# First attention layer: the first transposes of blocks 6 and 7 placed inside the next turn's gate piece and token tile

## The chip, the cores and the metric

The kernel runs on one core of a Trainium2 chip. The metric is the device time of one execution in microseconds (us), taken as the median of several runs. Engines are named as in the profile: PE (matrix multiply), PEld (its weight loads), DVE (vector), ACT (scalar), POOL (GpSimd) and SP (the queue that issues the DMAs).

## The reference

Two groups of rows, a prompt of 1024 positions and a sample of 32 with 512 cached positions, go through two layers that share the weights. The change lies in the first layer's mixer, a differential attention. Cut to what matters here (8 heads of 2 x 64, `h` the normalised input):

```python
q, k, v, g = jnp.split(h @ w_in, 4, axis=-1)
q = _rope(q.reshape(b, t, A_HEADS, 2, A_DH), pos)
k = _rope(k.reshape(b, t, A_HEADS, 2, A_DH), pos)
...
s = jnp.einsum('bqhcd,bkhcd->bhcqk', qb, kf) * (A_DH ** -0.5)
mask = k_chunk[None, :] <= (qpb // CHUNK)[:, None]
pr = jax.nn.softmax(jnp.where(mask, s, NEG_INF), axis=-1)
w = pr[:, :, 0] - lam * pr[:, :, 1]
o = jnp.einsum('bhqk,bkhe->bqhe', w, vf)
...
o = _rmsnorm(o, sub_g) * (1.0 - lam_init)
o = o.reshape(b, t, A_WIDTH) * jax.nn.silu(g)
```

The output projection, a gated addition of a second input, a second layer of another kind of attention with the same additions, and a final normalisation follow. The change touches none of these.

## The kernel before

`diff_layer` runs eight head groups one after another (`groups`, `body(r, more)`, where `more` is false in the last). Each engine has its own program, and the engines meet at semaphores alone. Within a group every program walks through the same turns, `for j in range(2, LAST + 1)` with `LAST = 13`. A turn carries pieces of different stages of the pipeline, written out by hand in a fixed order per engine.

There are nine units u: eight blocks of 128 query rows (0 to 7; block u sees (u + 1) x 128 keys) and the sample (8). For each unit the work passes through these steps:

- `scores(u)` on PE, in turn u + 2;
- `maxima(u)` on DVE and `probs(u, c)` on ACT (exponentials of the two softmaxes), in turn u + 3;
- `combine(u)` on DVE (L655): it scales the second softmax (L663) and adds the first to it (L665, SCALAR_TENSOR_TENSOR), which is the tile `la_p`. The semaphore `weights` tells that it is done;
- `turn_weights(u, g)` on PE (L855, instruction line L868): it transposes `la_p` in sets of up to four 128 x 128 pieces into one PSUM bank, `la_third`. Set g = 0 stood at the end of turn u + 4, set g = 1 (blocks 4 to 7 alone have one) in the middle of turn u + 5;
- `move(u, g)` on ACT (L459, line L473): it copies the bank to `la_wt`. The next set waits for that (`moved`), since there is only one bank;
- `values(c)` on PE (L871, line L892): weights times values, for blocks 0 to 3 in turn 8, for blocks 4 to 7 at the end of turn 12, and for the sample in turn 13.

To give PE work between these steps, turns 9 to 11 also carry the gate's projection (`gate_project(c, ks)`, L905: three column pieces of 352, each with eight steps `ks` of three matmuls at L107 on `la_wg_high` and `la_wg_low`), and turns 12 and 13 carry the next group's first two token tiles (`project(ahead, t, ks)`, L794: eight steps of three matmuls at L107 on `area`). Both are cut into `EARLY` (steps 0 to 4) and `LATE` (steps 5 to 7), and other work stands between the two. In the last group there is no next tile.

The next tile's weights come into `area` in two parts while the group runs: ACT rounds a slice (L427), then POOL forms the rest (`split_w`, L773). Steps 0 to 2 are split in turn 9, 3 to 5 in turn 10, 6 and 7 in turn 11. `project(ahead, 0, ...)` waits before each of its steps k for POOL's split of that step. POOL also multiplies the gate (`gate_product(c)`, L769), in turns 10 to 12 and ahead of that turn's splits; it waits for ACT's last gate step (`gate_sigmoid`, L492), which waits for DVE's `gate_soft(c)` (L689), which stands behind `combine` in DVE's program. ACT's order in turn 11 is: the sample's exponentials, `move(6, 1)`, `gate_log(1)`, `gate_raw(2)`, `gate_sigmoid(1)`, `move(7, 0)`, the rounding of slices 6 and 7. In turn 12: `move(7, 1)`, `gate_log(2)`, `gate_sigmoid(2)`, `move(8, 0)`. DVE's in turn 12: the clamp of gate piece 2, `combine(8)`, `gate_soft(2)`, `finish(0)` (L677).

In the last group ACT and DVE split the first two blocks of the output weights in place of the next tile's slices (`OUT_AT`, turns 9 and 10; ACT L562, DVE L713), on ACT directly behind that turn's `move(j - 4, 0)`.

Of the kernel before, what the change touches and what calls it, by code (L numbers as in the profile page):

```python
# [32 lines left out]
NT = SEQ // P  # L33
# [69 lines left out]
def three(pe, out, a, b, start, stop, **kw):  # L103

    pairs = [(a[0], b[0]), (a[1], b[0]), (a[0], b[1])]
    for n, (x, y) in enumerate(pairs):
        last = pe.matmul(out, x, y, start=start and n == 0, stop=stop and n == 2, **kw)  # L107
    return last
# [153 lines left out]
def diff_layer(nc, top, name, h, w_in, k_past, v_past, k_out, v_out, o_dram, w_out, ident, neg_lam, gain, cos, sin, stage, area, pj):  # L262
# [7 lines left out]
    GATE_AT = {9: 0, 10: 1, 11: 2}  # L270
# [7 lines left out]
    def groups_of(u):  # L278

        if u == NT:  # L280
            return [(0, PB + 1)]
        return [(k, min(4, u + 1 - k)) for k in range(0, u + 1, 4)]
# [4 lines left out]
    with ExitStack() as ctx:  # L287
# [503 lines left out]
        def _(pe):  # L791
            start_credits(pe, {x: s for x, s in S.items() if x != "w_low"}, 4, 5)

            def project(at, t, ks):  # L794
                n = TILES[t][1]
                rows = slice(t * P, t * P + n)
                for k in ks:
                    if t == 0:
                        pe.wait_ge(S["w_low"], at.nth("w_low", k + 1))
                    last = three(pe, pj[0:n, t % 2, 0:NQ], [x[:, k, rows] for x in h], [x[:, k, :] for x in w],  # L800
                                 k == 0, k == KT - 1, skip_group_check=True)
                if ks[-1] == KT - 1:
                    last.then_inc(S["pj_tok"], 1)

            def turn(at, t):
                pe.wait_ge(S["rope"], at.nth("rope", t + 1))
                n = TILES[t][1]
                if n < P:
                    pe.sem_inc(S["pe_tick"], 1)
                for x in range(2):  # L810
                    last = pe.transpose(pj[:, t % 2, x * P:x * P + n], tok[0:n, t, x * P:(x + 1) * P], ident[0:n, 0:n])
                last.then_inc(S["turned"], 1)

            EARLY, LATE = range(0, 5), range(5, KT)
# [9 lines left out]
            def body(r, more):  # L824
                at, ahead = Count(table, r), Count(table, r + 1)
# [29 lines left out]
                def turn_weights(u, g):  # L855
                    q0, n, nk = UNITS[u]
                    pe.wait_ge(S["weights"], at.nth("weights", u + 1))
                    pe.wait_ge(S["moved"], at.nth("moved", moves_before(u) + g))
                    if u == 0:
                        pe.wait_ge(S["log"], at.before("log"))  # L860
                    if n < P:
                        pe.sem_inc(S["pe_tick"], 1)
                    k0, nb = groups_of(u)[g]
                    bank = third[:, 0:nb * n].rearrange("p (b n) -> p b n", n=n)
                    for b in range(nb):
                        k = (k0 + b) * P
                        rows = min(P, nk - k)
                        last = pe.transpose(bank[0:rows, b, :], p[0][u % 3][0:n, k:k + rows], ident[0:n, 0:n])  # L868
                    last.then_inc(S["w_turned"], 1)

                def values(c):  # L871
                    c0, cn = CHUNKS[c]

                    if c == 0:
                        pe.wait_ge(S["normed"], at.before("normed"))
                    elif c == 1:
                        pe.wait_ge(S["normed"], at.nth("normed", 1))
                    else:
                        pe.wait_ge(S["probs"], at.all("probs"))

                    pe.wait_ge(S["moved"], at.nth("moved", moves_before((4, 8, 9)[c])))
                    out = sums_bank(c)
                    if c == 2:
                        for b in range(PB):
                            pe.matmul(out[:, 0:cn], vp[:, b, :], wt_sample[:, b, :], start=b == 0, stop=False)
                        last = pe.matmul(out[:, 0:cn], tok[0:DEC, NT, 2 * P:], wt_sample[0:DEC, PB, :],
                                         start=False, stop=True)
                    else:
                        blocks = 4 * (c + 1)
                        for b in range(blocks):  # L890
                            q = max(0, b * P - c0)
                            last = pe.matmul(out[:, q:], tok[:, b, 2 * P:], wt[:, b, q:],  # L892
                                             start=b == 0, stop=b == blocks - 1)
                    last.then_inc(S["pv"], 1)

                def variance(c):
                    cn = CHUNKS[c][1]
                    pe.wait_ge(S["squared"], at.nth("squared", c + 1))
                    if c == 0:
                        pe.wait_ge(S["turned_low"], at.all("turned_low"))  # L900
                    elif c == 1:
                        pe.wait_ge(S["moved"], at.all("moved"))
                    pe.matmul(var_bank(c)[:, 0:cn], mean[:, :], squares(c), start=True, stop=True).then_inc(S["var"], 1)

                def gate_project(c, ks):  # L905
                    if ks[0] == 0:
                        if c == 0:
                            pe.wait_ge(S["gw_low"], at.all("gw_low"))
                            pe.wait_ge(S["turned_low"], at.nth("turned_low", NT))
                        elif c == 1:  # L910
                            pe.wait_ge(S["log"], at.nth("log", 1))
                        else:
                            pe.wait_ge(S["g_raw"], at.nth("g_raw", 1))
                    for k in ks:
                        last = three(pe, gate_bank(c), [x[:, k, :] for x in wg],
                                     [x[:, k, gate_cols(c)] for x in h], k == 0, k == KT - 1, skip_group_check=True)
                    if ks[-1] == KT - 1:
                        last.then_inc(S["g_ready"], 1)

                def free_bank(t):  # L920

                    if t < 2:
                        pe.wait_ge(S["g_raw"], at.nth("g_raw", t + 2))
                    else:
                        pe.wait_ge(S["turned_low"], at.nth("turned_low", t - 1))
                    if t == PAST_AT + 1:
                        pe.wait_ge(S["past_low"], at.all("past_low"))

                for j in range(2, LAST + 1):
                    if j <= 8:  # L930
                        free_bank(j)
                        project(at, j, EARLY)
                    if j in GATE_AT:
                        gate_project(GATE_AT[j], EARLY)
                    if more and j >= 12:
                        free_bank(j - 12)
                        project(ahead, j - 12, EARLY)
                    if j <= 9:
                        turn(at, j - 1)
                    if more and j == 13:  # L940
                        turn(ahead, 0)
                    if 0 <= j - 5 <= NT and len(groups_of(j - 5)) > 1:
                        turn_weights(j - 5, 1)
                    if j == 13:
                        values(2)
                    if j <= 8:
                        project(at, j, LATE)
                    if j in GATE_AT:
                        gate_project(GATE_AT[j], LATE)
                    if more and j >= 12:  # L950
                        project(ahead, j - 12, LATE)
                    if j == PAST_AT:
                        pe.wait_ge(S["past"], at.nth("past", 32))
                        pe.wait_ge(S["turned_low"], at.nth("turned_low", PAST_AT))
                        for b in range(PB):
                            last = pe.transpose(past_bank[:, b * P:(b + 1) * P], kp[:, b, :], ident[:, :])
                        last.then_inc(S["past_turned"], 1)
                    if j == 9:
                        variance(0)
                    if 0 <= j - 2 <= NT:  # L960
                        scores(j - 2)
                    if 0 <= j - 4 <= NT:
                        turn_weights(j - 4, 0)
                    if j == 8:
                        values(0)
                    if j == 12:
                        values(1)
# [1389 lines left out]
```

## Time and profile before

| | |
|---|---|
| median of 3 runs | 2026.64 us |
| lowest and highest | 2021.52 and 2026.65 us |
| the profiled execution, whole time | 2027.47 us |
| its span | 2025.6 us (1.87 us of its time lie around it) |
| PE busy, share of the span | 1897.3 us, 94% |
| DVE, ACT, POOL busy | 1122.7, 1069.4, 387.3 us |
| mean granted TensorE clock | 0.975 of full speed |

The eight groups of the first attention lie at about 60 to 710 us of the span, and follow each other every 81.2 us. In the windows of 80 us between 80 and 640 us, PE is busy for 77.4 of 80 us and the granted clock is 1.00.

In the rows, times are us from the span's start; a timeline row gives start, duration, engine, line, operation, output <- inputs, shapes and count, and in brackets the engine's idle time just before and what ended it. Matmuls overlap, so the distance from one start to the next tells their price. A matmul's modelled end and POOL's spans are rough.

### The profile page before, as it was taken

How to read it: one execution, taken by the hardware profiler on the slowest of the kernel's cores; microseconds unless marked ns; L12 is line 12 of the kernel's file. 1: busy time of each engine (PE TensorE's matmuls, PEld its weight loads, DVE VectorE, ACT ScalarE, POOL GpSimd, SP SyncE). 2: the span in 40 equal slices, each digit the busy share in tenths (PEclk: the TensorE clock that was granted, in tenths of full speed). 3: DMA queues.
4: the chain of work that ended last, by engine and by line, in shares of the span. 5: the costliest groups of instructions: out<-in, count | busy, mean ns of one | idle time of the engine just before them, and what ended most of it. 6: DMA issues, size and time to landing. Idle time of an engine off the chain costs nothing. (4 is left out here: it accounts for less than half of the span.)

```text
span 2025.6 us, 31736 instructions
## 1 busy us (share of the span) xinstructions
PE 1897.3 (94%) x11429; PEld 1623.9 (80%) x11429; DVE 1122.7 (55%) x2269; ACT 1069.4 (53%) x2556; POOL 387.3 (19%) x597
## 2 busy tenths in 40 slices
PE   4999999999999899997799999999999999889996
PEld 4887878878878699986678787878787778689995
DVE  5556455565564532455165657575657575753555
ACT  5456455454554522454266667566657575732335
POOL 0132222321322000265001111110111011100341
PEclk7999999999999899998899999999999999999999
DMA  4121112111211242211111111111101111243113
GB/s 153 55 66 38 48 51 61 59 49 51 72 38 48 97 122 81 68 63 49 52 48 37 49 38 48 38 48 38 56 30 59 31 55 45 80 125 95 53 52 125
DMA packets 161803, 125.07 MB, mean 62 GB/s; under 512 B 10992, under 2 KB 152624, under 8 KB 161648
## 3 DMA queue, kind: packets, MB, share of 16 engines
q1 hardware_dynamic: 160784, 122.85, 19.8%
q8 instruction: 92, 1.51, 0.3%
q14 instruction: 63, 0.52, 0.1%
q10 hardware_dynamic: 864, 0.20, 0.0%
HBM read 89.49 MB, written 33.52 MB: 61 GB/s over the span
## 5 line engine op out<-in xcount | busy, mean ns | idle before, releaser
L107 PE MATMUL pj<-area,h_high 128*128 128x384 f32 (+1 forms) x2304 | 660.9, 349 | 25.8 <-issue 11.3
L107 PEld LDWEIGHTS pj<-area,h_high 128*128 128x128 f32 (+1 forms) x2304 | 408.2, 181 | 49.2 <-issue 11.4
L107 PE MATMUL pj<-area,h_low 128*128 128x384 f32 (+1 forms) x1152 | 390.8, 339 | 0.0
L107 PEld LDWEIGHTS pj<-area,h_low 128*128 128x128 f32 (+1 forms) x1152 | 210.3, 183 | 8.5
L1530 POOL TENSOR_TENSOR lb_o<-lb_o,lb_keep 128x512 f32<-128x512 f32 (+3 forms) x80 | 77.2, 965 | 603.0 <-ACT lb_keep L1230 596.4
L1375 DVE SCALAR_TENSOR_TENSOR lb_s<-lb_sc,lb_m 128x512 f32<-128x512 f32 (+4 forms) x200 | 109.9, 550 | 73.9 <-ACT lb_m L1211 73.9
L1201 ACT ACTIVATE lb_m<-lb_sc 128x512 f32<-128x512 f32 (+4 forms) x200 | 87.7, 486 | 81.0 <-PE lb_sc L1612 41.0
L455 ACT ACTIVATE la_p<-la_sc,la_nm 128x128 f32<-128x128 f32 (+5 forms) x144 | 105.8, 737 | 33.8 <-DVE la_nm L652 32.9
L1406 DVE CAST lb_s_high<-lb_s 128x512 fp32r<-128x512 f32 (+1 forms) x192 | 105.5, 549 | 25.7 <-DVE lb_s L1375 0.5
L1408 DVE TENSOR_TENSOR lb_s_low<-lb_s,lb_s_high 128x512 fp32r<-128x512 f32 (+1 forms) x192 | 115.5, 601 | 6.6
L650 DVE TENSOR_REDUCE la_mx<-la_sc 128x1 f32<-128x128 f32 (+5 forms) x144 | 107.6, 747 | 2.2
L1425 DVE TENSOR_TENSOR lb_o<-lb_acc,lb_o 128x512 f32<-128x512 f32 (+3 forms) x80 | 42.3, 529 | 112.8 <-PE lb_acc L1670 112.1
L107 PE MATMUL pj<-h_high,area 128*128 128x384 f32 (+1 forms) x384 | 94.4, 331 | 6.0 <-PEq L93 4.7
L1186 ACT ACTIVATE lb_tok<-pj,norm_token 128x128 f32<-128x128 f32 (+1 forms) x72 | 26.4, 367 | 133.2 <-PE pj L107 133.2
L1634 PEld LDWEIGHTS lb_sc<-lb_s_high,lb_tri 128*128 128x128 f32 x192 | 36.4, 189 | 73.6 <-issue 70.1
L1206 ACT ACTIVATE lb_m<-lb_m 128x512 f32<-128x512 f32 (+4 forms) x200 | 93.8, 522 | 0.3
L1211 ACT ACTIVATE lb_m<-lb_m 128x512 f32<-128x512 f32 (+4 forms) x200 | 93.6, 520 | 0.3
L1221 ACT ACTIVATE lb_a<-lb_sc 128x512 f32<-128x512 f32 (+4 forms) x200 | 87.8, 489 | 7.8 <-PE lb_sc L1634 5.9
L107 PE MATMUL mix_b_g<-mix_b_x_high,area 128*128 128x384 f32 (+1 forms) x384 | 91.7, 324 | 0.0
L107 PE MATMUL mix_a_g<-mix_a_x_high,area 128*128 128x384 f32 (+1 forms) x384 | 91.3, 323 | 0.0
L1634 PE MATMUL lb_sc<-lb_s_high,lb_tri 128*128 128x512 f32 (+1 forms) x192 | 76.6, 407 | 13.6 <-DVE lb_s_low L1408 13.5
L757 POOL TENSOR_TENSOR la_ra<-la_tok,cos 128x64 f32<-128x64 f32 (+1 forms) x72 | 23.1, 321 | 335.6 <-ACT la_tok L438 335.6
(307 smaller groups left out, 4491.7 us busy)
## 6 DMA issues: line engine op xcount, KB each, us to landing
stage<-in_a_w_in SPq DMA_DIRECT2D x60, 192.0 KB, 3.5
stage<-in_b_w_in SPq DMA_DIRECT2D x60, 192.0 KB, 3.0
stage<-in_ple_w_gate SPq DMA_DIRECT2D x22, 512.0 KB, 3.8
h_low<-o_t SPq DMA_DIRECT2D x14, 528.0 KB, 6.2
mix_b_xs<-x_mid SPq DMA_DIRECT2D x8, 528.0 KB
lift_xt<-in_x SPq DMA_DIRECT2D x8, 512.0 KB, 4.4
stage<-in_a_w_in SPq DMA_DIRECT2D x16, 256.0 KB, 5.1
out_ak<-la_tok SPq DMA_DIRECT2D x8, 512.0 KB, 3.3
```

What stands on the lines that cost most here:

```text
L107: last = pe.matmul(out, x, y, start=start and n == 0, stop=stop and n == 2, **kw)
L455: act.activation(p[c][u % (3 - c)][0:n, 0:nk], scores_of(u)[:, c, :], ACT.Exp, bias=nm[0:n, u % 2, c:c + 1], accum_out=sums[0:n, u % 2, c: ...
L650: dve.reduce_max(mx[0:n, u % 2, c:c + 1], x[:, c, :], AX.X).then_inc(S["dve_link"], 1)
L1201: act.activation(x, slot, ACT.Abs).then_inc(S["size"], 1)
L1206: act.activation(x, x, ACT.Exp, scale=-1.0).then_inc(S["exp"], 1)
L1211: act.activation(x, x, ACT.Ln, bias=1.0).then_inc(S["log"], 1)
L1221: act.activation(a, slot, ACT.Exp).then_inc(S["a"], 1)
L1375: ins = dve.scalar_tensor_tensor(out=sp, in0=slot, scalar=0.0, in1=x, op0=ALU.max, op1=ALU.add)
L1406: dve.tensor_copy(high, sp).then_inc(S["high"], 1)
L1408: dve.tensor_tensor(low, sp, high.bitcast(F32), ALU.subtract).then_inc(S["low"], 1)
L1530: pool.tensor_tensor(out, out, kept[n % 2][:, q:], ALU.mult).then_inc(S["scaled"], 1)
L1634: last = pe.matmul(slot, tri[:, :], part, **add)
```

## The change

The set g = 0 of block 6 moves from the end of turn 10 to turn 11, behind the first two steps of gate piece 2; that of block 7 moves from the end of turn 11 to turn 12, behind the first three steps of the next group's tile 0 (in the last group to the start of turn 12, with nothing ahead of it). Only PE's program differs; the other engines' programs, all waits and all buffers are as they were.

```diff
-                    if j in GATE_AT:
+                    if j in GATE_AT and j != 11:
                         gate_project(GATE_AT[j], EARLY)
-                    if more and j >= 12:
-                        free_bank(j - 12)
-                        project(ahead, j - 12, EARLY)
+                    if j == 11:
+                        gate_project(GATE_AT[j], EARLY[0:2])
+                        turn_weights(6, 0)
+                        gate_project(GATE_AT[j], EARLY[2:])
+                    if j == 12:
+                        if more:
+                            free_bank(0)
+                            project(ahead, 0, EARLY[0:3])
+                        turn_weights(7, 0)
+                        if more:
+                            project(ahead, 0, EARLY[3:])
+                    if more and j == 13:
+                        free_bank(1)
+                        project(ahead, 1, EARLY)
...
-                    if 0 <= j - 4 <= NT:
+                    if 0 <= j - 4 <= NT and j - 4 not in (6, 7):
                         turn_weights(j - 4, 0)
```

On PE, at the border of turns 10 and 11 of the first group, where `la_sc` is the sample's scores, `la_p00` the weights of block 6 and `la_wg` the gate's weights:

```order
 L851 MATMUL la_sc<-la_qk_low,la_qk_high 32x32 x2
+L107 MATMUL pj<-h_high,la_wg_high 128x352
+L107 MATMUL pj<-h_high,la_wg_low 128x352
+L107 MATMUL pj<-h_low,la_wg_high 128x352
+L107 MATMUL pj<-h_high,la_wg_high 128x352
+L107 MATMUL pj<-h_high,la_wg_low 128x352
+L107 MATMUL pj<-h_low,la_wg_high 128x352
 L868 MATMUL la_third<-ident,la_p00 128x128 x4
```

Six matmuls of the gate now stand ahead of block 6's four transposes instead of behind them; this is so in all eight groups.

On PE, at the border of turns 11 and 12 of the first group, where `la_p10` is the weights of block 7 and `area` the next group's projection weights:

```order
 L107 MATMUL pj<-h_low,la_wg_high 128x352
+L107 MATMUL pj<-area,h_high 128x384
+L107 MATMUL pj<-area,h_low 128x384
+L107 MATMUL pj<-area,h_high 128x384 x2
+L107 MATMUL pj<-area,h_low 128x384
+L107 MATMUL pj<-area,h_high 128x384 x2
+L107 MATMUL pj<-area,h_low 128x384
+L107 MATMUL pj<-area,h_high 128x384
 L868 MATMUL la_third<-ident,la_p10 128x128 x4
 L107 MATMUL pj<-area,h_high 128x384
```

Nine matmuls of the next tile now stand ahead of block 7's first four transposes, in seven groups. Steps 3 to 7 of that tile, block 7's second set and the sample's set follow in the order they had.

On PE of the changed kernel, at the border of turns 11 and 12 of the last group, where `la_p20` is the sample's weights:

```order
L107 MATMUL pj<-h_low,la_wg_high 128x352
L868 MATMUL la_third<-ident,la_p10 128x128 x8
L868 MATMUL la_third<-ident,la_p20 128x32 x4
L868 MATMUL la_third<-ident,la_p20 32x32
L892 MATMUL la_acc<-la_wt,la_tok 128x512 x5
```

Here block 7's two sets stand behind the gate's last matmul with nothing between or ahead of them, as they did before.

## Rows read from the trace of the kernel before

**Rows 1.** The page, busy time, share and instructions of each engine
```profile
PE 1897.3 (94%) x11429; PEld 1623.9 (80%) x11429; DVE 1122.7 (55%) x2269; ACT 1069.4 (53%) x2556; POOL 387.3 (19%) x597
```

**Rows 2.** PE's waits, 60 to 710 us: total, times, longest
```profile
PE la_third L868 <- DVE la_p L665: 19.6, 16, 1.7
```

**Rows 3.** Timeline of PE, second group, turns 10 to 12
```profile
193.75 0.66 PE L868 MATMUL la_third<-ident,la_p 128*128 128x128 f32 x4 [0.74 <-DVE la_p L665]
...
200.28 0.66 PE L868 MATMUL la_third<-ident,la_p 128*128 128x128 f32 x4 [1.70 <-DVE la_p L665]
200.69 0.42 PE L107 MATMUL pj<-area,h_high 128*128 128x384 f32 x1
...
202.53 0.34 PE L107 MATMUL pj<-area,h_low 128*128 128x384 f32 x1
...
204.72 0.64 PE L107 MATMUL pj<-area,h_high 128*128 128x384 f32 x2
...
205.64 0.46 PE L868 MATMUL la_third<-ident,la_p 32*128 32x32 f32 x5
```

**Rows 4.** Timeline of PEld, second group, tile 0's last step
```profile
204.92 0.19 PEld L107 LDWEIGHTS pj<-area,h_high 128*128 128x128 f32 x1 [0.18 <-POOL area L773]
```

**Rows 5.** Tile `area`, PEld, 60 to 700 us: idle until, total, times
```profile
  POOL area L773: 1.1, 7
```

**Rows 6.** Timeline of POOL, second group, turns 10 to 12
```profile
195.65 3.50 POOL L773 TENSOR_TENSOR area<-stage,area 128x384 fp32r<-128x384 f32 x3
...
201.27 0.95 POOL L769 TENSOR_TENSOR la_gate<-la_gate,la_gtmp 128x352 f32<-128x352 f32 x1 [2.12 <-ACT la_gtmp L492]
202.18 1.22 POOL L773 TENSOR_TENSOR area<-stage,area 128x384 fp32r<-128x384 f32 x1
...
203.36 1.50 POOL L773 TENSOR_TENSOR area<-stage,area 128x384 fp32r<-128x384 f32 x1
```

**Rows 7.** Timeline of DVE, second group, turns 11 and 12
```profile
198.32 1.91 DVE L665 SCALAR_TENSOR_TENSOR la_p<-la_p,la_sums 128x1024 f32<-128x1024 f32 x1
200.15 0.51 DVE L689 SCALAR_TENSOR_TENSOR la_gtmp<-la_gate,la_gtmp 128x352 f32<-128x352 f32 x1
...
202.55 1.43 DVE L665 SCALAR_TENSOR_TENSOR la_p<-la_p,la_sums 32x544 f32<-32x544 f32 x1
205.59 0.53 DVE L689 SCALAR_TENSOR_TENSOR la_gtmp<-la_gate,la_gtmp 128x352 f32<-128x352 f32 x1 [1.61 <-ACT la_gtmp L487]
```

**Rows 8.** Timeline of ACT, second group, turns 10 to 12
```profile
194.57 0.58 ACT L473 ACTIVATE la_wt<-la_third 128x512 f32<-128x512 f32 x1
...
200.70 0.50 ACT L492 ACTIVATE la_gtmp<-la_gtmp 128x352 f32<-128x352 f32 x1 [1.29 <-DVE la_gtmp L689]
...
201.58 0.93 ACT L427 ACTIVATE area<-stage 128x384 fp32r<-128x384 f32 x2
204.04 0.60 ACT L473 ACTIVATE la_wt<-la_third 128x512 f32<-128x512 f32 x1 [1.53 <-PE la_third L868]
```

**Rows 9.** Timelines of PE, ACT and DVE, last group, turns 10 to 12
```profile
684.80 0.64 PE L107 MATMUL pj<-h_high,la_wg_high 128*128 128x352 f32 x1
...
686.71 0.49 PE L107 MATMUL pj<-h_high,la_wg_high 128*128 128x352 f32 x1
...
692.36 0.66 PE L868 MATMUL la_third<-ident,la_p 128*128 128x128 f32 x4 [1.44 <-DVE la_p L665]
...
696.11 8.85 PE L892 MATMUL la_acc<-la_wt,la_tok 128*128 128x512 f32 x16
...
685.18 0.60 ACT L473 ACTIVATE la_wt<-la_third 128x512 f32<-128x512 f32 x1 [0.57 <-PE la_third L868]
...
686.76 1.23 DVE L713 TENSOR_TENSOR area<-stage,area 128x1024 fp32r<-128x1024 f32 x1 [2.08 <-ACT area L562]
...
691.02 1.28 DVE L665 SCALAR_TENSOR_TENSOR la_p<-la_p,la_sums 128x1024 f32<-128x1024 f32 x1
```

**Rows 10.** Stretch of the last group: length; busy PE, PEld, DVE, ACT, POOL; clock; DMA
```profile
695.35:702.18 6.83, 6.66 (x12) 3.05 (x13) 3.65 (x5) 3.37 (x7) 0.93 (x1) 0.50 0.95 387
```

## The prediction

> **What bounds the kernel now.** I read the page's busy times first: PE is at work for 94% of the span [rows 1], so little can be won by moving PE's own work, and the question is what PE waits for. The waits of PE over the first attention answer it: it stands still in front of the transposes L868 until DVE's L665 has finished a block's weights, 16 times, 19.6 us in all [rows 2]. The timeline of PE shows which: in each of the eight groups block 6's first set waits about 0.74 us and block 7's about 1.70 us [rows 3]; eight times 2.44 is the 19.5 us. So the edit aims at the right place, and its ceiling is 19.6 us, 1.0% of the time.
>
> Next I ask what else ends late just behind that place. The weight loads of PE show a short wait there, 0.18 us for POOL's split L773, in front of the last step (k = 7) of the next group's tile 0 [rows 4]. Summed over the layer it is only 1.1 us, but there are seven of them, one for every group that has a next tile [rows 5]. POOL's last split ends at 203.36 + 1.50 = 204.86 and the load starts at 204.92 [rows 4, 6]. PE reaches its step 7 just as POOL releases it. This small row decides the case: whatever PE gains ahead of step 7 is given back in front of it, unless POOL's split comes earlier as well.
>
> Does it? The chain behind it can be followed through three engines. DVE ends block 7's L665 at 198.32 + 1.91 = 200.23 and then runs the gate's L689 until 200.66 [rows 7]; ACT's L492 starts at 200.70 [rows 8]; POOL's product L769 at 201.27, and its two splits at 202.18 and 203.36 [rows 6]. The transposes that PE waits for hang on the same 200.23 (they start at 200.28). So PE's stall and POOL's split have one origin, DVE's chain, which starts from scores that PE computes well ahead of the moved pieces. Nothing in the change makes this chain start earlier.
>
> **The change part by part, groups with a next tile (seven).** *Block 6's set.* PE is done with the sample's scores at 193.75 - 0.74 = 193.01 and now does six gate matmuls first. The same six take 1.91 us in the last group, where the clock is half [rows 9], so about 0.96 here, and the set starts at about 194.0, with its input ready: the wait of 0.74 is gone. *Block 7's set.* All PE work up to it is 0.74 earlier, so PE would stand at 200.28 - 1.70 - 0.74 = 197.84 where it stood at 198.58. Nine matmuls of tile 0 come next. From 200.69 to 202.53 there are ten distances of 0.184 us [rows 3], so nine cost 1.66, and the set is reached at 199.50. Its input is there at 200.28 as before, so 0.78 us of wait remain. PE is then 1.66 us ahead: the ceiling for these groups is 7 x 1.66 = 11.6 us, not 17.
>
> *Behind it.* Steps 3 and 4, block 7's second set and step 5 follow at once. Step 6 needs the first of POOL's last two splits (ends about 203.4), step 7 the second (204.86). Tile 0's last first matmul came at about 204.90 before [rows 3, 4] and comes at 204.92 now: the 1.66 us are spent there, in two waits of PE for POOL. From the sample's set at 205.64 on [rows 3] all is as it was, and the period of 81.2 us stays. Value taken: 0, with the bounds 0 (POOL holds exactly) and -1.66 (POOL does not hold).
>
> *A price on the way.* Block 6's first set ends at about 194.0 + 0.66 = 194.7, and ACT's copy of it, which started at 194.57 [rows 8], starts 0.1 us later. Behind the copy ACT rounds slices 3 to 5, and POOL's three splits at 195.65 [rows 6] follow it. They run beside block 7's `combine`, and its L665 takes 1.91 us here [rows 7] against 1.28 in the last group, where POOL splits nothing [rows 9]. So a shift of POOL can become a shift of DVE's chain, and that sets step 7. Bounds 0 and 0.3 us (the whole shift of the transposes); I take 0.1, since ACT was busy until 194.57 anyway: 7 x 0.1 = 0.7 us.
>
> **The last group.** There is no next tile, so block 7's set gets nothing in front of it and its wait for DVE stays. But block 6's set is moved behind six matmuls at half clock, 686.71 - 684.80 = 1.91 us [rows 9]. ACT's copy waits for PE there (0.57 us, at 685.18); behind it ACT rounds the output weights, and DVE waits 2.08 us for that at 686.76, ahead of block 7's `combine` at 691.02 [rows 9]. None of these has slack, so block 7's set moves from 692.36 to 694.3 and the values from 696.11 to 698.0. The values run at half clock until 702.18 [rows 10]; starting 1.9 later, they do 1.9 us less at half speed, which gives 0.95 back if the clock rises at the same time as before. I take +1.0 us, with the bounds 0.9 and 1.9 (the stretch of half clock moves along).
>
> **The sum** is 7 x 0 + 0.7 + 1.0 = +1.7 us: 2027.47 + 1.7 = 2029.2 us against the profiled execution (span 2025.6 and 1.87 around it). That execution is 0.8 us above the median of the runs shown, 2026.64, so I predict 2028.3 us: no difference that can be told (a measurement of this kernel tells about 0.3%, 6.1 us, from no change).
>
> **A rival that ends faster: POOL does not hold step 7.** Then the 1.66 us stay in seven groups: 2028.3 - 11.6 = 2016.7 us, 0.5% faster. For it speaks that POOL's spans are rough, and that PE came to step 7 at nearly the same moment by its own pace: in before the wait cost PE some 0.02 us, so the row could be a coincidence. Against it: the load follows the end of POOL's span by 0.06 us, and PEld is put down as waiting for POOL in all seven groups [rows 5]. The Trainium skill ("Perfetto Trace Analysis", GPSIMD Engine Instruction) advises to time such instructions by the distance of their starts and not by their spans. By that distance, 203.36 - 202.18 = 1.18 us, the last split would end at 204.54, and the sum would be 7 x 0.32 = 2.2 us lower, -0.5 us in all; the load at 204.92 speaks for the span's end.
>
> **A rival that ends slower: DVE and POOL collide in a new place.** Block 7's second set now starts at 200.69 + 6 x 0.184 = 201.8 and ends at 202.5, so ACT's copy moves from 204.04 [rows 8] to about 202.5, just behind its rounding (201.58 + 0.93). What follows on ACT comes 1.54 us earlier, and DVE's L689 of gate piece 2 moves from 205.59 to 204.05 [rows 7]: into POOL's last split, which still has 0.81 us to run, and a second such operation of DVE follows it. If both go at half speed while they overlap, the split ends 0.8 us later and PE's step 7 with it: 7 x 0.8 = 5.6 us on top of the forecast, 2033.9 us, 0.36% slower. It counts as slower from (6.1 - 1.7) / 7 = 0.63 us per group.
>
> How such a collision is shared can be read at two places. The sample's L665 runs from 202.55 to 203.98 [rows 7], and the split that starts at 203.36 takes 1.50 us [rows 6]: 0.88 us after DVE is done, close to the 3.50 / 3 = 1.17 us per split of the earlier three, some of which waited too. That is a split which stood until DVE was through and then ran undisturbed. Block 7's L665, 0.63 us longer than in the last group, overlaps POOL's third split for 195.65 + 3.50 - 198.32 = 0.83 us [rows 6, 7]; at half speed it would have lost 0.42, standing still up to 0.83, and it is nearer to the middle. In both places the one that came second lost. By that reading the new L689 comes second, waits some 0.8 us itself, and nobody waits for it: POOL loses nothing. The Trainium skill ("SBUF — State Buffer", Who interferes with whom) states it as a rule: where a DVE instruction has two inputs in SBUF and GpSimd reads SBUF, the second to issue is blocked until the first is done. By that rule the sum stays +1.7 us, by half speed it is +7.3; the two places above fit the rule better, so this rival keeps a small chance.
>
> **How the numbers follow.** Forecast 0.74: POOL holds step 7, within 0.3%. Faster rival 0.10. Slower rival 0.16, with the last group's upper bound in it. The rivals lie outside the 0.3% on their sides, so faster is 0.10, same 0.74, slower 0.16. The predicted time is the forecast's. The range: the forecast's own bounds are +0.9 (no shift of POOL) to +4.0 (7 x 0.3 + 1.9), that is 2027.5 to 2030.6; the runs before differ by 5.1 us (2021.52 to 2026.65), so I put its foot at 2022.5; upward it reaches into the slower rival, to 2033.5.
>
> **What the profile after would show.** Right: the wait of L868 for L665 falls from 19.6 us to roughly 7 x 0.8 for block 7 plus about 3 in the last group, block 6's waits are gone, and in exchange PE waits for POOL's L773 in front of steps 6 and 7 of tile 0, some 0.6 and 0.9 us in each of seven groups; the period of the groups stays at 81.2 to 81.4 us. The right total with POOL's last split ending later relative to block 7's L665 would speak for the collision. In the last group block 7's set should start near 694.3. Wrong: a period near 79.6 us (POOL did not hold) or of 82 us and more (the collision costs POOL).

## The result and the profile after

| | before | changed |
|---|---|---|
| median of 20 runs | 2024.49 us | 2028.70 us |
| lowest and highest | 2018.12 and 2028.74 | 2022.31 and 2034.98 |
| ratio, 95% interval | | 1.0024 [1.0015, 1.0033] |
| span of the profiled execution | 2025.6 us | 2024.0 us |

The changed kernel is 0.24% slower, some 4.9 us of 2025 with the interval 3.0 to 6.7. That is inside 0.3%, but it is no zero. The absolute time of 2028.3 us was met to 0.4 us by luck, since with more runs the median of before came out 2.2 us lower than the one the sum was added to; the change was forecast at +1.7 us.

The two profiled spans differ the other way round. From its first matmul on, the second layer takes 1036 to 1044 us in the profiles of this study, whatever the first attention does, so the traces are compared within the first attention.

PE's waits of the changed kernel, 60 to 712 us (total, times, longest), answer [rows 2]:

```profile
PE la_third L868 <- DVE la_p L665: 10.8, 8, 3.9
PE pj L107 <- POOL area L773: 7.7, 14, 0.7
PE la_sc L851 <- ACT la_p L455: 3.2, 1, 3.2
```

The wait for block weights has fallen from 19.6 to 10.8 us, and a new one has come, for POOL's split, 14 times in seven groups (the third line is 3.2 us in before as well). On the weight loads, where the standstill shows longer, it is 12.2 us where it was 1.1 [rows 5]. The timeline of PE, second group (start, duration, ..., idle before and what ended it), answers [rows 3]:

```profile
193.88 0.60 PE L868 MATMUL la_third<-ident,la_p 128*128 128x128 f32 x4
...
200.26 0.66 PE L868 MATMUL la_third<-ident,la_p 128*128 128x128 f32 x4 [0.98 <-DVE la_p L665]
...
203.41 0.44 PE L107 MATMUL pj<-area,h_high 128*128 128x384 f32 x1 [0.45 <-POOL area L773]
...
204.85 0.44 PE L107 MATMUL pj<-area,h_high 128*128 128x384 f32 x1 [0.65 <-POOL area L773]
...
205.58 0.46 PE L868 MATMUL la_third<-ident,la_p 32*128 32x32 f32 x5
```

Block 6's set starts without a wait. Block 7's starts where it did (200.26 against 200.28), 0.98 us of its wait left. Then PE waits in front of step 6 and again in front of step 7, and step 7 starts within 0.1 us of where it stood. The two waits on the weight loads, and the rest of the chain on POOL, DVE and ACT, answer [rows 4] and [rows 6 to 8]:

```profile
203.41 0.19 PEld L107 LDWEIGHTS pj<-area,h_high 128*128 128x128 f32 x1 [0.77 <-POOL area L773]
...
204.85 0.19 PEld L107 LDWEIGHTS pj<-area,h_high 128*128 128x128 f32 x1 [0.97 <-POOL area L773]
...
202.15 2.65 POOL L773 TENSOR_TENSOR area<-stage,area 128x384 fp32r<-128x384 f32 x2
...
202.52 1.41 DVE L665 SCALAR_TENSOR_TENSOR la_p<-la_p,la_sums 32x544 f32<-32x544 f32 x1
204.02 1.17 DVE L689 SCALAR_TENSOR_TENSOR la_gtmp<-la_gate,la_gtmp 128x352 f32<-128x352 f32 x1
...
194.52 0.60 ACT L473 ACTIVATE la_wt<-la_third 128x512 f32<-128x512 f32 x1
...
202.47 0.60 ACT L473 ACTIVATE la_wt<-la_third 128x512 f32<-128x512 f32 x1
```

POOL's two splits end at 204.80; before it was 204.86. ACT's copy of block 7's second set came forward from 204.04 to 202.47, and with it DVE's L689 from 205.59 to 204.02. That instruction now takes 1.17 us instead of 0.53. It started with 0.78 us of POOL's split still to run and lost 0.64 of them, while POOL lost nothing.

What the groups cost can be read from the start of the values of blocks 4 to 7 (the ninth L892 matmul of each group): the distance from group to group is the period. The table holds it for all profiles of this study, the changed kernel's two beside the experiments below. The third column counts the periods with a stretch in which PE's granted clock is half; the last column runs from the seventh group's values to the layer's last square (L499), which takes in the last group.

| kernel | six periods, us | at half clock | last group, us |
|---|---|---|---|
| before | 81.21 to 81.24 | none | 93.99 |
| before again (e11) | 81.22 to 81.27 | none | 94.46 |
| changed | five 81.26 to 81.31, one 83.00 | 1 | 95.63 |
| changed again (e4) | five 81.27 to 81.30, one 82.97 | 1 | 93.81 |
| not in the last group (e3) | five 81.26 to 81.30, one 82.95 | 1 | 92.85 |
| block 7 alone (e2) | five 81.18 to 81.21, one 82.92 | 1 | 93.64 |
| block 6 alone (e1) | three 81.30 to 81.34, three 82.51 to 82.58 | 3 | 95.66 |
| block 6 alone, not last (e10) | three 81.28 to 81.32, three 82.55 to 82.66 | 3 | 92.94 |
| before, short splits (e5) | 81.10 to 81.15 | none | 94.41 |
| changed, short splits (e6) | 79.67 to 79.69 | none | 95.60 |
| changed, early rounding (e7) | 80.45 to 80.50 | none | 95.46 |
| early, not last (e8) | 80.45 to 80.50 | none | 93.99 |
| early, copy first (e9) | 80.26 to 80.29 | none | 92.84 |

In the undisturbed groups the changed kernel's period is 0.05 us longer than before: the whole gain of 1.66 us is given back. What it loses lies in two other places: one group in six that runs 1.7 us longer, and the last group.

The long group of the first profile shows in stretches of the trace (length; busy time and instructions of PE, PEld, DVE, ACT, POOL; granted clock; DMA), the same place of the program in the changed kernel and, second fence, in the kernel before:

```profile
527.00:531.40 4.40, 3.30 (x20) 2.30 (x19) 3.81 (x4) 2.78 (x9) 3.41 (x4) 1.00 0.02 6
531.40:534.80 3.40, 3.40 (x5) 1.35 (x4) 0.69 (x1) 0.60 (x3) 0.39 (x1) 0.50 0.17 47
```

```profile
526.90:531.30 4.40, 4.40 (x29) 3.85 (x28) 2.73 (x4) 2.22 (x6) 2.88 (x3) 1.00 0.02 4
531.30:534.70 3.40, 3.40 (x9) 1.52 (x8) 1.19 (x2) 1.04 (x4) 0.93 (x1) 1.00 0.11 32
```

Around steps 5 to 7 of tile 0 PE had been busy all the time; now it is busy 3.30 of 4.40 us there, and behind that the granted clock is 0.50, at 1.2 of 2.4 GHz. The values that follow run at half speed: five matmuls in 3.4 us where there were nine.

### The profile page after: what moved, and what is told of

It reads as the page before. It is cut to its first block and busy times, and to the rows that moved or that the text cites. A ratio compares the mean times of both kernels' runs of the same rounds, so it can differ in the third digit from the quotient of the medians.

```text
span 2024.0 us, 31736 instructions
## 1 busy us (share of the span) xinstructions
PE 1898.4 (94%) x11429; PEld 1621.4 (80%) x11429; DVE 1124.9 (56%) x2269; ACT 1070.3 (53%) x2556; POOL 387.8 (19%) x597
## 5 line engine op out<-in xcount | busy, mean ns | idle before, releaser
L107 PEld LDWEIGHTS pj<-area,h_high 128*128 128x128 f32 (+1 forms) x2304 | 408.4, 181 | 59.8 <-POOL area L773 12.2
L107 PE MATMUL pj<-h_high,area 128*128 128x384 f32 (+1 forms) x384 | 94.2, 331 | 5.9 <-PEq L93 4.7
L1217 ACT ACTIVATE lb_m<-lb_m 128x512 f32<-128x512 f32 (+4 forms) x200 | 93.8, 523 | 0.3
L1222 ACT ACTIVATE lb_m<-lb_m 128x512 f32<-128x512 f32 (+4 forms) x200 | 93.6, 520 | 0.3
L633 DVE TENSOR_TENSOR la_qk_low<-pj,la_qk_high 128x256 fp32r<-128x256 f32 (+1 forms) x72 | 28.8, 401 | 106.7 <-ACT la_qk_high L442 106.7
```

The lines of the kernel that those rows point to most:

```text
L1217: act.activation(x, x, ACT.Exp, scale=-1.0).then_inc(S["exp"], 1)
L1222: act.activation(x, x, ACT.Ln, bias=1.0).then_inc(S["log"], 1)
```

## The experiments

**The two moves apart.** Block 6's set alone is moved in e1; from the changed kernel's code, block 7's goes back to the end of turn 11:

```diff
-                            project(ahead, 0, EARLY[0:3])
-                        turn_weights(7, 0)
-                        if more:
-                            project(ahead, 0, EARLY[3:])
+                            project(ahead, 0, EARLY)
...
-                    if 0 <= j - 4 <= NT and j - 4 not in (6, 7):
+                    if 0 <= j - 4 <= NT and j - 4 != 6:
                         turn_weights(j - 4, 0)
```

Block 7's alone is moved in e2; block 6's goes back to the end of turn 10:

```diff
-                    if j in GATE_AT and j != 11:
+                    if j in GATE_AT:
                         gate_project(GATE_AT[j], EARLY)
-                    if j == 11:
-                        gate_project(GATE_AT[j], EARLY[0:2])
-                        turn_weights(6, 0)
-                        gate_project(GATE_AT[j], EARLY[2:])
...
-                    if 0 <= j - 4 <= NT and j - 4 not in (6, 7):
+                    if 0 <= j - 4 <= NT and j - 4 != 7:
                         turn_weights(j - 4, 0)
```

> Only block 6's first set is moved; block 7's stands at the end of turn 11 as before. Theory (POOL's split pins the seven groups, the loss sits in the last group): block 6's wait of 0.74 us goes over into block 7's wait (about 2.4 us instead of 1.7 in the second group), the period stays at 81.2 to 81.3 us, the last group keeps its loss of about 1.7 us, so +1.5 to +2.5 us against the kernel before, more where the granted clock falls behind the longer wait. Rival (the new overlap of DVE's gate step with POOL's last split costs every group): that overlap does not arise here, so about +1.7 us, all of it in the last group.

> Only block 7's first set is moved; block 6's stands at the end of turn 10 as before. Theory: block 7's wait of 1.7 us becomes two waits for POOL ahead of steps 6 and 7 of tile 0, the period stays at 81.2 us, and the last group is as before: 0 to +0.5 us in all, plus 1.7 us for each stretch of half clock that falls into a group. Rival (overlap of DVE and POOL costs every group): the overlap is here as in the changed kernel, so 0.4 to 0.6 us per group, +3 to +4 us.

Measured: e1 1.0042 [1.0027, 1.0057], some 8.5 us slower; e2 1.0015 [1.0003, 1.0026], 3 us. PE's waits in e1, then in e2 (total, times, longest):

```profile
PE la_third L868 <- DVE la_p L665: 21.5, 8, 3.8
```

```profile
PE la_third L868 <- DVE la_p L665: 8.7, 9, 3.3
PE pj L107 <- POOL area L773: 7.7, 14, 0.6
```

In e1 the sum of the waits is no smaller than before (21.5 us against 19.6), but it lies in 8 waits in place of 16: block 6's wait went over into block 7's. In e2 block 7's wait became the two for POOL. In neither is the undisturbed period more than about 0.1 us off. So the rival of a new collision that every group pays falls: e2 has the overlap of DVE and POOL (L689 takes 1.17 us there too), and its undisturbed period is 81.2 us. But what e1 lost is far above the 1.5 to 2.5 us expected, where a falling clock stood as a possibility without a price. Its periods say where it is: three groups of 82.5 us, each with a stretch at half clock. With 3 x 1.25 for these, 0.5 for six periods and 1.7 for the last group, 6 of the 8.5 us are found in the trace; where the rest lies is open. In that profile the first scores start 2.2 us later than in before as well; this lies ahead of the change, in the phase before the groups, and is not claimed for it.

**The last group.** Both sets moved in seven groups, the last in the old order (e3, its edit against the changed kernel), beside the changed kernel again (e4):

```diff
-                    if j in GATE_AT and j != 11:
+                    if j in GATE_AT and (j != 11 or not more):
                         gate_project(GATE_AT[j], EARLY)
-                    if j == 11:
+                    if more and j == 11:
...
-                    if j == 12:
-                        if more:
-                            free_bank(0)
-                            project(ahead, 0, EARLY[0:3])
+                    if more and j == 12:
+                        free_bank(0)
+                        project(ahead, 0, EARLY[0:3])
                         turn_weights(7, 0)
-                        if more:
-                            project(ahead, 0, EARLY[3:])
+                        project(ahead, 0, EARLY[3:])
...
-                    if 0 <= j - 4 <= NT and j - 4 not in (6, 7):
+                    if 0 <= j - 4 <= NT and (not more or j - 4 not in (6, 7)):
                         turn_weights(j - 4, 0)
```

> Both sets are moved in the seven groups with a next tile; the last group has the order of before. Theory: the last group's loss of about 1.7 us is gone, the period stays at 81.3 us, so +0.3 us and 1.7 us for each stretch of half clock in the groups, 0 to +3 us in all. Rival (every group pays): +3.5 to +4 us, only little less than the changed kernel.

> The changed kernel once more, beside the others on the same chip. Theory: the period of the groups is 81.3 us wherever the granted clock is full, the last group is 1.7 us longer than before, and the rest of its loss is stretches of half clock in the seven groups, which need not fall into the same group as in the first profile. Rival: the period is longer in all groups.

Measured: e3 1.0007 [0.9994, 1.0019], e4 1.0017 [1.0005, 1.0029]. The intervals overlap, but the 1.7 us between the medians (2026.86 and 2028.58) is what the theory asked for, and the trace agrees in direction: over the five profiles in which block 6's set is moved in the last group (changed, e4, e1, e6, e7) the last column of the table is 95.2 us in the mean, over the eight others 93.6. The difference of 1.6 us is not steady, since in e4, where the gate's matmuls of the last group ran at full clock, the group is no longer than before. Part of it is the clock: in the last group it is half for 13.7 us in four of the five profiles (all but e4) and in four of the eight others (before, e11, e5, e8), and for 10.2 us in the rest. Like for like the difference is 1.4 us among those with 13.7 (95.6 against 94.2) and 0.7 among those with 10.2 (93.8 against 93.1). Whether the moved set itself makes the longer half clock more likely, 13 profiles do not say. PE and the wait it ends in, last group of the changed kernel's first profile, answers [rows 9]; behind it the same place before, with the sample's set that follows:

```profile
687.29 1.05 PE L868 MATMUL la_third<-ident,la_p 128*128 128x128 f32 x4
...
695.56 1.11 PE L868 MATMUL la_third<-ident,la_p 128*128 128x128 f32 x4 [3.92 <-DVE la_p L665]
```

```profile
684.03 1.12 PE L868 MATMUL la_third<-ident,la_p 128*128 128x128 f32 x4
...
695.52 0.66 PE L868 MATMUL la_third<-ident,la_p 32*128 32x32 f32 x5 [1.00 <-DVE la_p L665]
```

From block 6's set to block 7's it is 8.27 us now, 692.36 - 684.03 = 8.33 before: the whole chain behind ACT's copy moved along with the set. PE waits 3.92 us in front of block 7's where it waited 1.44; in before's second profile (e11), where more of the gate's matmuls ran at full clock, that wait was 2.81 us already, so not all of the longer wait is the change's.

**Is the stretch of half clock the waits' doing?** Block 6 alone, not in the last group (e10), and the kernel before once more (e11); the edits are those above.

> Only block 6's set is moved, and only in the seven groups with a next tile. Theory (the one long wait of about 2.4 us lets the granted clock fall behind it in some groups, 1.25 us each time, three times in the first profile of block 6 alone): period 81.3 us in groups at full clock and 82.5 us in two to four others, +3 to +5.5 us against the kernel before. Rival (the loss of block 6 alone was the last group and the start of the kernel): +0.5 us, no stretch of half clock in the seven groups.

> The kernel before once more, beside the others, for its profile. Theory: its two shorter waits, 0.74 and 1.70 us with work between them, leave the granted clock full in all seven groups, period 81.2 us throughout, and the time is that of the kernel before. Rival (stretches of half clock fall there by chance, whatever the waits): one or more of them between 60 and 660 us here too.

Measured: e10 1.0039 [1.0024, 1.0053], some 7.9 us slower (4.9 to 10.7; 5.2 between the medians) where 3 to 5.5 were expected; e11 0.9995 [0.9982, 1.0008]. The six periods of e10 hold 4.4 us of its loss; where the rest lies is open. In e10 the half clock falls into the second, fourth and sixth of six periods, the same three as in e1. One of them, the wait and then the stretches around it:

```profile
446.98 1.12 PE L868 MATMUL la_third<-ident,la_p 128*128 128x128 f32 x4 [2.54 <-DVE la_p L665]
```

```profile
442.00:446.70 4.70, 2.43 (x17) 2.12 (x15) 4.56 (x8) 4.07 (x11) 3.81 (x4) 1.00 0.15 44
446.70:450.10 3.40, 3.12 (x11) 3.13 (x12) 3.29 (x7) 1.92 (x4) 1.83 (x2) 0.50 0.00 0
```

PE stands still for 2.54 us in one piece, and the clock is half as it starts again. Counted over the profiles, a group fell to half clock in 6 of 12 periods with one wait of about 2.5 us (e1, e10), in 4 of 24 with two waits for POOL close together (changed, e3 and e4, with 0.98 us ahead of them; e2 without that), in 0 of 18 with 0.74 and 1.70 and work between (before, twice, and e5 below), and in 0 of 24 of e6 to e9, whose waits are shorter in sum. Before, the changed kernel and block 6 alone make PE stand still for about as long in sum, 2.4, 2.1 and 2.5 us a group on PE's rows; what differs is how close together it lies. Six of 12 against none of 18 is hardly chance, though both profiles of block 6 alone fall in the same three groups; four of 24 could still be. That the closeness decides is read from these counts alone. Why one group falls and the next, with the same waits, does not, the runs do not say.

**Does POOL's split take the gain back?** Short splits for slices 6 and 7, in before (e5) and in the changed kernel (e6). They treat 32 of 384 columns and leave the rest of these low parts out:

```diff
-                    pool.tensor_tensor(w[1][:, k, :], raw_w(k), w[0][:, k, :].bitcast(F32), ALU.subtract).then_inc(S["w_low"], 1)
+                    n = 32 if k >= 6 else NQ
+                    pool.tensor_tensor(w[1][:, k, 0:n], raw_w(k)[:, 0:n], w[0][:, k, 0:n].bitcast(F32),
+                                       ALU.subtract).then_inc(S["w_low"], 1)
```

> The kernel before, but POOL's splits of slices 6 and 7 treat 32 of 384 columns in groups 1 to 7 (the rest of these low parts keeps older values, so that part of the product is left out). It takes the hold in front of tile 0's step 7 away and nothing else that PE waits for. Theory (PE's two waits for DVE are the only cost of before here; POOL costs it about 0.02 us a group): within 1 us of the kernel before in the first attention, period 81.2 us.

> The changed kernel with the same short splits of slices 6 and 7. Theory (POOL's last split takes back what the moved sets give): with that hold gone the 1.66 us stay in each of seven groups, period about 79.6 us, 10 to 11.6 us less than the changed kernel, 7 to 9 us (0.35 to 0.45%) below the kernel before. Rival (the moved sets only trade one wait for another of DVE's or ACT's): period stays at 81.2 us, no difference from the changed kernel.

Measured: e5 0.9990 [0.9980, 1.0001], e6 0.9952 [0.9936, 0.9969]. Only with the moved sets does the short split bring something: the period falls from 81.13 (e5) to 79.67 us (e6), 1.6 below the changed kernel. All that is left of waits of PE in these turns is this one (second group of e6; the transposes are L870 there, and L873 and L874 in the kernels below, since lines were added above them):

```profile
198.72 0.66 PE L870 MATMUL la_third<-ident,la_p 128*128 128x128 f32 x4 [0.99 <-DVE la_p L665]
```

This settles the main step of the prediction. POOL's last split holds the seven groups, and without that hold the moved sets are worth 1.5 us a group (against e5) to 1.6 (against the changed kernel), close to the 1.66 that the sum gave as their ceiling.

**A version that keeps the gain.** In turn 11 ACT stands idle before the gate's last step, so the rounding of slices 6 and 7 can go there, and POOL's splits ahead of the gate's product (e7; e8 the same with the last group in its old order). The first two pieces are ACT's, ahead of `gate_sigmoid` and behind `move`, the last two POOL's:

```diff
+                    if more and j == 11:
+                        for k in WEIGHTS_AT[j]:
+                            split_w(r + 1, k)
...
-                    if more and j in WEIGHTS_AT:
+                    if more and j in WEIGHTS_AT and j != 11:
...
-                    if j - 1 in GATE_AT:
+                    if j - 1 in GATE_AT and j != 11:
                         gate_product(GATE_AT[j - 1])
...
+                    if j == 11:
+                        gate_product(GATE_AT[j - 1])
```

> The changed kernel, all work kept; in turn 11 ACT rounds slices 6 and 7 ahead of the gate's last step instead of behind block 7's copy, and POOL splits them ahead of the gate's product. ACT stands idle from about 199.4 to 200.7 us in the second group, so POOL's splits can begin right after block 7's combine and end near 202.5 instead of 204.9. Theory: PE's waits ahead of steps 6 and 7 go, period about 79.6 us, 9 to 11.6 us below the changed kernel. Rival (a load of slice 7 that lands at about 200 us, or DVE and POOL in each other's way, takes its place): period 80.5 us or more.

> As the run before, but the last group keeps the order of the kernel before. Theory: another 0.5 to 1.9 us below that run, about 9 to 12 us (0.45 to 0.6%) below the kernel before. Rival as in that run.

Measured: e7 0.9983 [0.9973, 0.9993], e8 0.9977 [0.9964, 0.9990]; both beat the kernel before, by less than I expected, with a period of 80.5 us in place of 79.6. Second group of e7, in PE, then POOL, DVE and ACT:

```profile
202.90 0.63 PE L873 MATMUL la_third<-ident,la_p 128*128 128x128 f32 x4 [0.64 <-ACT la_wt L473]
...
200.14 2.47 POOL L776 TENSOR_TENSOR area<-stage,area 128x384 fp32r<-128x384 f32 x2 [0.73 <-ACT area L427]
...
200.42 1.32 DVE L692 SCALAR_TENSOR_TENSOR la_gtmp<-la_gate,la_gtmp 128x352 f32<-128x352 f32 x1
...
201.77 0.50 ACT L492 ACTIVATE la_gtmp<-la_gtmp 128x352 f32<-128x352 f32 x1 [1.30 <-DVE la_gtmp L692]
202.17 0.58 ACT L473 ACTIVATE la_wt<-la_third 128x512 f32<-128x512 f32 x1
```

The waits for POOL are gone, but the rival came true in part. POOL's splits start 0.28 us ahead of the gate's step on DVE, which now takes 1.32 us instead of 0.51; ACT's last gate step waits for that, block 7's copy stands behind it, and PE waits 0.64 us for the copy. So in e9, built on e8, ACT copies first:

```diff
                             split_w(r + 1, k)
+                        move(7, 0)
                     if j - 1 in GATE_AT:
                         gate_sigmoid(GATE_AT[j - 1])
...
-                    if 0 <= j - 4 <= NT:
+                    if 0 <= j - 4 <= NT and not (more and j == 11):
                         move(j - 4, 0)
```

> As the run with early rounding and the last group in its old order, and in turn 11 ACT copies block 7's first set ahead of the gate's last step instead of behind it. In that run the copy waited for the gate's step, the step for DVE, and DVE for POOL's early splits, and PE waited 0.64 us for the copy. Theory (PE's own pace is the limit once neither POOL nor the copy holds it): period 79.7 us instead of 80.5, another 5 to 5.6 us less, 10 to 13 us (0.5 to 0.65%) below the kernel before. Rival (POOL's early splits end too late for step 7 all the same): period stays near 80.5 us.

Measured: 0.9969 [0.9958, 0.9981], 2018.67 us against 2025.48, some 6.3 us less where 10 to 13 were expected. It has the shortest period of the versions that keep all work; by its time alone it cannot be told from e8. The period is 80.27 us, not 79.7: POOL and DVE still meet, DVE's combine of the sample comes later, and PE now waits for that:

```profile
204.71 0.43 PE L874 MATMUL la_third<-ident,la_p 32*128 32x32 f32 x5 [0.56 <-DVE la_p L669]
```

## Why the prediction held, and where its sum fell short

- *The pin on POOL* was right, and it was the step that decided. Two waits in front of steps 6 and 7 came as forecast (0.77 and 0.97 us on the weight loads, 0.6 and 0.9 forecast), the period stayed, and e6 shows that 1.5 to 1.6 of the 1.66 us are there as soon as POOL does not hold them. The faster rival falls with it. The small row [rows 5], 1.1 us in all, told it: that a wait is short does not mean that it is far from binding.
- *Block 7's remaining wait* was forecast at 0.78 us and is 0.98. PE came to it about 0.2 us earlier than I counted. With 3.92 us in the last group, where about 3 was forecast, the waits for block weights are 10.8 us and not the 8.6 of the signs.
- *One reading of [rows 2]* was wrong, without changing the sum. The 16 waits are not two in each of eight groups: the last group has none for block 6's set, 1.44 us for block 7's and 1.00 for the sample's. That these two are 2.44 as well is chance. What the moved sets could win at most was thus some 17.1 us and not 19.6.
- *The price on the way*, forecast at 0.1 us a group, is 0.05 on the period; ACT's copy moved by 0.07 us against the scores.
- *The collision of DVE and POOL* took place where I put it, at 204.02 us, and ended as the two places of [rows 6, 7] had it: the later one, DVE's L689, lost 0.64 us where about 0.8 was reckoned, POOL's splits took 2.65 us where they had taken 2.68. The rule in the Trainium skill ("SBUF — State Buffer", Who interferes with whom), that the second to issue is blocked until the first is done, agrees, and e7 shows the same once more (1.32 us). The slower rival, as it was worked out, falls.
- *The last group* was forecast at +1.0 us with the bounds 0.9 and 1.9. The chain was right: in the first profile block 7's set comes 1.3 us later behind the seventh group's values than before, and the group's own values 1.9, the shift that was forecast (695.56 in place of 694.3 holds 1.9 us that the earlier groups had lost). The difference of the means is 1.6, like for like in the clock 0.7 to 1.4, and single profiles lie 0.2 to 2.0 above the others' mean.
- *What the sum lacked* is a term for the granted clock in the seven groups. I had it fall in the last group alone, since there it was in the trace of before, and took for granted that waits of the same sum leave it as it is elsewhere. One group in six lost 1.7 us in each of the changed kernel's two profiles. With 0.05 x 7 and 1.4 to 1.6 for the last group this gives 3.5 to 3.7 us, inside the interval of both measurements (3.0 to 6.7 and 1.0 to 5.9), where the forecast of 1.7 is outside the first; with the 0.7 it gives 2.8, just below the first.

## To carry to other kernels

Before moving work into a wait, look for the next wait behind it, however short: if another engine already releases the same engine a few instructions later, and both hang on one origin, the gain ends there, and the order on that other engine (here ACT's rounding and POOL's splits) has to be moved with it. Move a set of transposes only where the copy behind it has room: in the last group the same move put up to 1.9 us into a chain that had none. And spread waits may cost less than the same waits in one piece.

## What the runs showed of the hardware that was not expected

A single wait of 2.54 us of PE, or shorter waits close together, was followed by a stretch at 1.2 GHz in some groups (3 of 6 periods with the single wait in both of its profiles, 1 of 6 in each profile with the shorter ones), while 0.74 and 1.70 us with work between them was not in any of 18. Moving block 6's set alone (e1), which left the sum of the waits nearly as it was (21.5 us against 19.6), thus cost more than moving both: 2033.46 against 2028.58 us in the median, three stretches of half clock against one. Where DVE and POOL meet, the instruction that waits shows the wait inside its own duration (L689 1.17 and 1.32 us instead of 0.52), not as idle time in front of it, so no view of waits lists it.
